# Recurrence outputs written to the other row halves and issued in turn with the state's update, and new starting rounds for attention's items

## The chip, the cores and the metric

One NeuronCore of a Trainium2 chip runs the whole program. The time is the device time of one execution in microseconds (us), as the median of several runs. TensorE (PE in the profile, PEld for its weight loads) multiplies, VectorE (DVE), ScalarE (ACT) and GpSimd (POOL) work on vectors, SyncE (SP) issues DMAs. Each engine works off its own instructions in program order, and engines wait for one another by semaphores.

## The reference

Two blocks follow each other. The first has two layers over 1,040 tokens (16 of them learned). In each layer an input projection feeds two branches: an attention with 4 heads over all tokens, and a recurrence over 8 heads with a state of 64 x 64, run once forwards and once backwards in time; both go through an output product and a norm, and then through a mixture of 32 experts. The second block has a differential attention, a gated spatial mixing and a gated feed-forward part. Everything is in 32-bit floats. The change concerns the first block's recurrence and the attention beside it:

```python
def step(S, inp):
    r_t, w_t, k_t, v_t, kk_t, b_t = inp
    sa = jnp.einsum('bhvk,bhk->bhv', S, kk_t)
    S = S * w_t[:, :, None, :] - sa[..., None] * b_t[:, :, None, :] + v_t[..., None] * k_t[:, :, None, :]
    return S, jnp.einsum('bhvk,bhk->bhv', S, r_t)

def attend(blk):
    qn, qp = blk
    s = jnp.einsum('bqhd,bkhd->bhqk', qn, k_nope) + jnp.einsum('bqhd,bkd->bhqk', qp, k_pe)
    p = jax.nn.softmax(s.astype(jnp.float32) * scale, axis=-1).astype(v.dtype)
    return jnp.einsum('bhqk,bkhd->bqhd', p, v)
```

## The kernel before, in words

The program runs stage after stage: projections, then recurrence with attention (some 350 to 1,085 us for layer 0, some 2,155 to 2,875 us for layer 1), closing products, routing, experts, and then the second block.

**The recurrence in chunks.** Time is cut into 10 steps of 104 tokens (C), each of two chunks of 52 (H), for each direction d (0 forwards, 1 backwards). Two heads lie above each other in the 128 partitions: one in rows 0 to 63, the other in rows 64 to 127; a chunk's tokens take rows 0 to 51 and 64 to 115 (these slices are `ODD`, line 1185). Within a chunk the recurrence is solved with matrices. A step has phases 0 to 31 (`PHASES`, line 1177): 0 makes the gate inputs from the low-rank weights (line 1365, called lora here); 1 to 10 make decays, exponentials and scaled keys, on VectorE, ScalarE and GpSimd; 11 and 14 turn matrices over; 12 and 13 make the products of keys; 15 to 25 invert a triangular matrix in five levels, each with a first part (T by lm, gives XX) and a second part (XX by T, gives T); 26 to 28 and 29 to 31 are the two chunks: the right-hand side (`state_rows`, evicted to rh), the solve (evicted to uu), and then, in phases 28 and 31, the state's update and the outputs.

**Rounds.** 23 groups of phases make a step. `rounds()` (line 1218) issues one group of direction 0 and one of direction 1 in a round, direction 1 being 11 rounds behind (`STAGGER`). So when direction 0 is in its group r, direction 1 is in group r + 12 (or r - 11). Between the two directions' parts of a round stands attention's turn (the entry with None). The order in a round is direction 0, attention, direction 1; in rounds 0 to 3 of direction 0's step it is direction 1, attention, direction 0, since a direction in its first four groups goes last. All engines take this same order. Phases 28 and 31 come in rounds 19 and 22 for direction 0 and in rounds 7 and 10 for direction 1. The gate inputs come in round 0 for direction 0 and in round 11 for direction 1. Direction 1's level four is in rounds 1 and 2 (first and second part), direction 0's in rounds 13 and 14; direction 0's round 12 is the second part of level three.

**State's update and outputs.** In `scan_pe` (line 1356), part 2, the update's products go as 16 matmuls: for each of 4 pairs of heads j two accumulated products (tm by vt, tm by uu), each for both row halves. They read rows of one half and write partitions of the same half, so a matmul of the upper half and one of the lower half make a pair. Then a semaphore step tells VectorE, which adds the update to S (line 1625). After that come the outputs (`outputs`, line 1336): for each j three accumulated products (S by kr, v by Ak, uu by Ab), again for both halves, 24 matmuls, in the same halves. ScalarE evicts them to ys (line 1475, `take` in `scan_act`), and `scan_sp` (line 1662) stores ys by four DMAs a step and direction. A 32-bit matmul shows as two instructions in the trace, so a pair shows as 4. `state_rows` and the five levels mix straight and crossed halves (`quarters`, line 1318).

**Attention's items.** An item is one tile of queries (104 in layer 0, 128 in layer 1) of one head: 40 items in layer 0, 32 in layer 1. It takes six rounds from its start (`att_turn`, line 1711): first round, scores of two of three spans of keys (kn by qn, kpe by qp); second, the third span, and on VectorE the three maxima (line 1837); third, the exponentials on ScalarE; fourth, the turning of p on TensorE (consts by p) and its copies; fifth, p by v (v by pT); sixth, the division o on VectorE (line 1862), its square on ScalarE (line 1826) and the store. `item_starts` (line 1683) takes the starting rounds within a step from `STARTS` (four items in a step; layer 0, and steps 0 and 5 of layer 1) or `FEWER` (three items; the other steps of layer 1). In step 0 the first start is left out.

Of the kernel before, what the change touches and what calls it, by code (L numbers as in the profile page):

```python
# [19 lines left out]
H, HP = 52, 116  # L20
# [188 lines left out]
class Program:  # L209
# [20 lines left out]
    def place(self, o, width, dt, name):  # L230
        if (o, width, dt, name) not in self.tensors:
            self.tensors[o, width, dt, name] = self.nc.alloc_sbuf_tensor_at(
                f"{name}{len(self.tensors)}", [128, width], dt, offset=self.base + 4 * o)
        return self.tensors[o, width, dt, name][:, :]
# [54 lines left out]
def mms(e, mats):  # L289
    for out, a, b, start, stop in mats:  # L290
        made = e.matmul(out, a, b, start=start, stop=stop)  # L291
    return made
# [890 lines left out]
MASKS = {14: 0, 15: 1, 16: 2, 18: 3, 20: 4, 22: 5}  # L1183
BY_ACT = {2, 3, 8, 9} | {13 + 3 * lv for lv in range(4)} | {25 + 4 * x + n for x in range(2) for n in (0, 1, 3)}
ODD = [(slice(64 * o, 64 * o + 64), slice(64 * o, 64 * o + H)) for o in range(2)]


def scan_mem(P):
# [49 lines left out]
def chunk(d, step):  # L1238
    i = step if d == 0 else NT - 1 - step
    return slice(C * i, C * i + C)  # L1240


def half(d, step, ch):
    t0 = chunk(d, step).start + H * ch
    return slice(t0, t0 + H)
# [6 lines left out]
def scan_bank(P, d, step, use):  # L1252
    return P.ps[2 * d + use % 2]
# [32 lines left out]
def half_rows(o):  # L1286
    return slice(64 * o, 64 * o + H)
# [7 lines left out]
def side(lv, ch, j):  # L1295

    return (j ^ ch * lv) & 1
# [12 lines left out]
def split_columns(j):  # L1312

    at = 128 * (j % 2) + 64 * (j // 2)
    return slice(at, at + 64)


def quarters(js):

    return [(j, o, half_rows(o), half_rows(o ^ j % 2)) for j in js for o in range(2)]  # L1320


def state_rows(P, d, m, S, ch, v):

    mats, hs = [], slice(H * ch, H * ch + H)
    for js in ((0, 1), (2, 3)):
        for j, o, r, x in quarters(js):
            out = P.ps[2 * d + j % 2][x, 64 * (j // 2):64 * (j // 2) + 64]
            mats.append((out, m.kr[64 * o:64 * o + 64, j, 0, hs], S[64 * o:64 * o + 64, j, :], True, False))
        for j, o, r, x in quarters(js):  # L1330
            out = P.ps[2 * d + j % 2][x, 64 * (j // 2):64 * (j // 2) + 64]
            mats.append((out, m.ak[r, place(1, ch, j), 0, :], v[r, 64 * j:64 * j + 64], False, True))
    return mats


def outputs(ps, m, S, ch, v):

    mats, hs = [], slice(H * ch, H * ch + H)
    for j in range(4):
        jc, u = slice(64 * j, 64 * j + 64), place(1, ch, j)  # L1340
        mats += [(ps[r, jc], m.kr[q, j, 1, hs], S[q, j, :], True, False) for q, r in ODD]
        mats += [(ps[r, jc], m.ak[r, u, 1, :], v[r, jc], False, False) for q, r in ODD]
        mats += [(ps[r, jc], m.ab[r, u, 1, :], m.uu[r, split_columns(j)], False, True) for q, r in ODD]
    return mats


def turns(e, P, pairs):

    made = []
    for out, a in pairs:  # L1350
        n, p = a.shape[0], a.base_partition()
        made.append((out, a, P.K["ident"][p:p + n, p:p + n], True, True))
    return mms(e, made)


def scan_pe(e, P, li, d, step, ph):
    rw, pe, dv, ac, po = P.rw, P.c("scan_pe"), P.c("scan_dve"), P.c("scan_act"), P.c("scan_pool")
    m, sl, key = P.scan[d], chunk(d, step), (li, d, step)
# [9 lines left out]
    if ph == 11:  # L1368
        e.wait_ge(*dv.at(*key, "kr0"))
        b = scan_bank(P, d, step, 2)  # L1370
        turns(e, P, [(b[r, 256 * ch + 64 * j:256 * ch + 64 * j + 64], rw.v[q, j, half(d, step, ch)])
                   for ch in range(2) for j in range(4) for q, r in ODD]).then_inc(*pe.tick(*key, 2))
    if ph in (11, 14):
        k, use = (1, 3) if ph == 11 else (0, 8)
        b = scan_bank(P, d, step, use)
        if ph == 14:
            scan_free(e, P, li, d, step, use)
        e.wait_ge(*dv.at(*key, f"hb{k}"))
        turns(e, P, [(b[r, 256 * ch + 64 * j:256 * ch + 64 * j + 64], m.hb[q, k, j, H * ch:H * ch + H])
                   for ch in range(2) for j in range(4) for q, r in ODD]).then_inc(*pe.tick(*key, use))  # L1380
    if 12 <= ph < 14:
        e.wait_ge(*dv.at(*key, "kr1" if ph == 12 else "hb0"))
        mat = 1 if ph == 12 else 0
        for ch in range(2):
            use = 2 * ph - 20 + ch
            b, hs = scan_bank(P, d, step, use), slice(H * ch, H * ch + H)
            scan_free(e, P, li, d, step, use)
            at = [2 * H * (place(1, ch, j) // 4 * 2 + j // 2) for j in range(4)]
            mms(e, [(b[r, at[j]:at[j] + 2 * H].rearrange("p (a t) -> p a t", a=2),
                     m.hb[q, mat, j, hs], m.kr[q, j, :, hs], True, True) for j in range(4) for q, r in ODD]  # L1390
                ).then_inc(*pe.tick(*key, use))
# [9 lines left out]
    if 16 <= ph < 26:  # L1401
# [3 lines left out]
        mats = []  # L1405
        if not second:
# [6 lines left out]
            for n in range(4):  # L1413
                for k in range(2):
                    ch, i = divmod(n, 2)
                    j = 2 * i + side(lv, ch, k)
                    for o in range(2):
                        r, x = half_rows(o), half_rows(o ^ k)
# [3 lines left out]
        else:  # L1422
            e.wait_ge(*dv.at(*key, "ev", base))
            for n in range(4 if lv < 5 else 0):
                for k in range(2):
                    ch, i = divmod(n, 2)
                    j = 2 * i + side(lv, ch, k)
                    for o in range(2):
                        r, x = half_rows(o), half_rows(o ^ k)
                        mats.append((left[r, k, H * n:H * n + H], m.TT[x, turned_place(lv, ch, j), :],  # L1430
                                     m.XX[x, 4 * k + n, :], True, True))
            for j in range(4):
                for ch in range(2):
                    for o in range(2):
                        x, y = half_rows(o ^ side(lv, ch, j)), half_rows(o ^ side(lv + 1, ch, j))
# [3 lines left out]
    if ph >= 26:  # L1439
        x, part = divmod(ph - 26, 3)  # L1440
        ch, S, use = m.chunks[x], m.S[x], 25 + 4 * x
        if part == 0:
            if x == 0:
                e.wait_ge(*dv.at(*key, "T", 5))
                e.wait_ge(*ac.at(*key, "T", 5))
                e.wait_ge(*ac.at(*key, "ev", 2))
                e.wait_ge(*dv.at(*key, "ev", 7))
            else:
                e.wait_ge(*ac.at(*key, "ev", use - 1))
            e.wait_ge(*(dv.at(*key, "fS", x) if step or x else dv.at(li, d, "S0")))  # L1450
            mms(e, state_rows(P, d, m, S, ch, m.vt[:, ch, :])).then_inc(*pe.tick(*key, use))
        if part == 1:
            e.wait_ge(*ac.at(*key, "ev", use))
            mms(e, [(P.ps[2 * d + j % 2][r, 64 * (j // 2):64 * (j // 2) + 64], m.TT[c, 4 * ch + j, :],
                     m.rh[c, split_columns(j)], True, True) for j, o, r, c in quarters(range(4))]
                ).then_inc(*pe.tick(*key, use + 1))
        if part == 2:
            b = scan_bank(P, d, step, use + 2)
            mats = []
            for j in range(4):  # L1460
                jc = slice(64 * j, 64 * j + 64)
                mats += [(b[q, jc], m.tm[r, 0, ch, jc], m.vt[r, ch, jc], True, False) for q, r in ODD]
                mats += [(b[q, jc], m.tm[r, 1, ch, jc], m.uu[r, split_columns(j)], False, True) for q, r in ODD]
            e.wait_ge(*ac.at(*key, "ev", use + 1))
            mms(e, mats).then_inc(*pe.tick(*key, use + 2))
            mms(e, outputs(scan_bank(P, d, step, use + 3), m, S, ch, m.vt[:, ch, :])).then_inc(*pe.tick(*key, use + 3))


def scan_act(e, P, li, d, step, ph):
# [192 lines left out]
def scan_sp(e, P, li, d, step, ph):  # L1662
    if ph == 31:
        e.wait_ge(*P.c("scan_act").at(li, d, step, "ev", 32))
        y = P.T[f"y{d}"][chunk(d, step), :].rearrange("(c t) (j o n) -> t o c j n", c=2, o=2, n=64)
        for o in range(2):
            for ch in range(2):
                e.dma_start(y[:, o, ch], P.scan[d].ys[64 * o:64 * o + H, ch, :].rearrange("p (j n) -> p j n", j=4)
                            ).then_inc(*P.d(f"scan_y{d}_out").tick(li, step, 2 * o + ch))


# [4 lines left out]

STARTS = (2, 8, 13, 20)
FEWER = (2, 9, 17)  # L1680


def item_starts(li):

    made = []
    for q in range(NT + 1):
        places = STARTS if li == 0 or q in (0, 5) else FEWER
        made += [STEPS * q + at for at in places if q or at != STARTS[0]]
    return made[:4 * TILES_OF[li]]
# [183 lines left out]
def recur_sp(e, P, li):  # L1873
    for o in range(2):
        e.dma_start(P.att.kpe[64 * o:64 * o + 64, :], P.T["kp"][:, 1 - o]).then_inc(
            *P.d("att_kpe_in").tick(li, *(() if o else ("hi",))))
    for piece in range(PIECES):
        att_load(e, P, li, 0, piece)
    att_query(e, P, li, 0)
    att_query(e, P, li, 1)  # L1880
    for piece in range(PIECES):
        att_load(e, P, li, 1, piece)
    for n, part in rounds():
        if part is None:
            att_sp(e, P, li, n)
            close_head_sp(e, P, li, n - STEPS * NT)
        else:
            scan_sp(e, P, li, *part)


def recur_pe(e, P, li):
    for n, part in rounds():
        if part is None:
            att_pe(e, P, li, n)
            close_head_pe(e, P, li, n - STEPS * NT)
        else:
            scan_pe(e, P, li, *part)
# [2513 lines left out]
```

## Time and profile before

| what | value |
|---|---|
| median of 3 runs | 4873.55 us (4872.19 to 4876.98) |
| profiled execution: time, span | 4854.41 us, 4852.5 us |
| PE busy, share of the span | 4436.8 us, 91% |
| DVE, ACT, POOL busy | 3122.8 us (64%), 2157.3 us (44%), 1191.1 us (25%) |
| mean granted clock of TensorE | 0.961 of full speed |
| layer 0, one step of the recurrence | 71.3 us |
| layer 1, one step of the recurrence (three items) | 67.9 us |

The span is the time from the first to the last instruction of the profiled execution. Busy shares are means over all stages. In the recurrence many small matmuls run at once and their ends are modelled, so the start of the next burst says more than the busy time.

### The profile page before, as it was taken

Reading aid. Unit: us, or ns where it says so; the run is one execution under the profiler, and the core shown is the slowest. Engines: PE = TensorE matmul, PEld = TensorE weight load, DVE = VectorE, ACT = ScalarE, POOL = GpSimd, SP = SyncE. Lnnn points to the kernel's source line nnn. Section 1 sums busy time; section 2 is a strip of 40 time slices with the busy share of each in tenths; the row PEclk is TensorE's granted clock in tenths of the full one; section 3 lists DMA queues with packets and bytes.
Section 4 is the critical chain, followed back from the end, with each engine's and each line's share of the span. In section 5 each row is a group of like instructions: output and inputs, shape, how many; then the busy total and the mean of one; then the engine's idle time right before and its main releaser. Section 6 shows DMA issues by size and latency. Waiting matters only on the chain. (4 is left out here: it accounts for less than half of the span.)

```text
span 4852.5 us, 125717 instructions
## 1 busy us (share of the span) xinstructions
PE 4436.8 (91%) x55312; PEld 3779.0 (78%) x55312; DVE 3122.8 (64%) x4912; ACT 2157.3 (44%) x3962; POOL 1191.1 (25%) x863
## 2 busy tenths in 40 slices
PE   6989999999799969989999888899979889999999
PEld 6888888887588858878888877788767557888887
DVE  6436666669688974346666677888774476651752
ACT  2333444442388853334343432788742252331431
POOL 1003222322244510012222221444321001222221
PEclk9999999999899979999999998999989789999999
DMA  5411111133466674321111133666651003333332
GB/s 150 144 54 36 35 28 34 25 88 85 161 257 256 243 213 121 105 60 24 30 34 31 25 119 115 225 248 251 232 177 35 9 19 113 96 112 109 113 113 91
DMA packets 385989, 535.77 MB, mean 110 GB/s; under 512 B 117982, under 2 KB 310558, under 8 KB 358422
## 3 DMA queue, kind: packets, MB, share of 16 engines
q1 hardware_dynamic: 343349, 488.54, 31.0%
q0 software_dynamic: 40752, 33.95, 2.2%
q8 instruction: 439, 7.19, 0.6%
q10 hardware_dynamic: 1344, 5.24, 0.3%
q14 instruction: 105, 0.85, 0.1%
HBM read 569.43 MB, written 121.40 MB: 142 GB/s over the span
## 5 line engine op out<-in xcount | busy, mean ns | idle before, releaser
L291 PE MATMUL ps<-w_hi,xbT 128*128 128x512 f32 x1520 | 497.5, 398 | 19.1 <-DVE w L2860 19.1
L291 PE MATMUL ps<-hT,w_in 128*128 128x416 f32 (+1 forms) x2736 | 493.1, 338 | 4.1 <-DVE hT L3147 4.1
L291 PEld LDWEIGHTS ps<-hT,w_in 128*128 128x128 f32 x2736 | 456.8, 194 | 30.0 <-issue 19.2
L2860 DVE TENSOR_TENSOR w<-w,w_hi 128x2048 fp32r<-128x2048 f32 x190 | 425.4, 2277 | 2.2 <-ACT w_hi L2817 2.2
L1657 POOL TENSOR_TENSOR lm<-Ab,consts 116x416 f32<-116x416 f32 x240 | 256.6, 1077 | 407.3 <-PE ps L291 237.3
L2817 ACT ACTIVATE w_hi<-w 128x2048 fp32r<-128x2048 f32 x190 | 355.2, 1935 | 0.0
L291 PEld LDWEIGHTS ps<-w_hi,xbT 128*128 128x128 f32 x1520 | 287.3, 189 | 86.4 <-DVE w L2860 28.1
L291 PE MATMUL ps<-w,xbT 128*128 128x512 f32 x760 | 297.9, 392 | 0.0
L2891 DVE TENSOR_TENSOR w<-w,w_hi 128x2048 fp32r<-128x2048 f32 x95 | 221.6, 2333 | 95.6 <-ACT w_hi L2853 95.6
L291 PE MATMUL ps<-w_hi,actT 128*128 128x512 f32 x760 | 250.8, 391 | 4.9 <-DVE actT L2886 4.9
L291 PE MATMUL ps<-x1T,w_gate 128*128 128x512 f32 x1056 | 249.5, 392 | 3.0 <-DVE x1T L3834 1.6
L291 PE MATMUL ps<-x1T,w_up 128*128 128x512 f32 x1056 | 246.5, 389 | 0.0
L291 PE MATMUL ps<-w_down,act 128*128 128x512 f32 x1056 | 241.6, 391 | 2.8 <-POOL w_down L4060 2.8
L1600 DVE TENSOR_TENSOR XX<-ps,consts 116x416 f32<-116x416 f32 x200 | 117.4, 587 | 189.3 <-PE ps L291 189.0
L291 PEld LDWEIGHTS ps<-x1T,w_gate 128*128 128x128 f32 x1056 | 200.0, 190 | 45.6 <-issue 1.9
L291 PEld LDWEIGHTS ps<-w_down,act 128*128 128x128 f32 x1056 | 199.3, 189 | 44.9 <-POOL w_down L4060 3.3
L291 PEld LDWEIGHTS ps<-x1T,w_up 128*128 128x128 f32 x1056 | 198.2, 188 | 41.2
L4051 POOL TENSOR_TENSOR w_up<-w_up,w_up 128x1024 fp32r<-128x1024 f32 x44 | 116.4, 2646 | 458.0 <-ACT w_up L3973 458.0
L291 PE MATMUL ps<-w_out,mixT 128*104 128x512 f32 (+1 forms) x864 | 218.5, 407 | 10.4 <-DVE w_out L2198 5.8
L2806 POOL DMA_INDIRECT t_ys<-yo,slots x95 | 101.3, 1066 | 461.5 <-PE ps L298 371.0
L291 PEld LDWEIGHTS ps<-w_out,mixT 128*104 128x104 f32 (+1 forms) x864 | 152.0, 179 | 67.5 <-DVE w_out L2198 9.6
L794 POOL TENSOR_TENSOR w_in<-w_in,w_in 128x1024 fp32r<-128x1024 f32 x22 | 56.0, 2551 | 598.9 <-ACT w_in L809 598.9
(464 smaller groups left out, 10776.2 us busy)
## 6 DMA issues: line engine op xcount, KB each, us to landing
w<-in_moe_w_dram SPq DMA_DIRECT2D x192, 1024.0 KB, 12.4
w_gate<-in_w_gate_dram SPq DMA_DIRECT2D x44, 512.0 KB, 3.8
w_up<-in_w_up_dram SPq DMA_DIRECT2D x44, 512.0 KB, 3.8
w_down<-in_w_down_dram SPq DMA_DIRECT2D x44, 512.0 KB, 3.6
w_in<-in_w_in_dram SPq DMA_DIRECT2D x36, 512.0 KB, 4.2
w_out<-in_w_out_dram SPq DMA_DIRECT2D x24, 512.0 KB, 8.3
t_h<-x SPq DMA_DIRECT2D x20, 416.0 KB
kn<-t_kn SPq DMA_DIRECT2D x32, 260.0 KB, 3.6
```

The costliest lines, as they stand in the source:

```text
L291: made = e.matmul(out, a, b, start=start, stop=stop)
L794: e.tensor_tensor(w.lo, w.x, w.hf, ALU.subtract).then_inc(*count.tick(li, "lo", n))
L1600: e.tensor_tensor(m.XX[0:HP].rearrange("p (k u) t -> p k u t", k=2), both_banks(P, d, 0)[0:HP].rearrange("p k (u t) -> p k u t", t=H), bc( ...
L1657: e.tensor_tensor(m.LM[lv % 2][0:HP], m.ab[0:HP, :, 0, :], bc(m.lmask[0:HP, H * lv:H * lv + H].unsqueeze(1), [HP, 8, H]), ALU.mult).then_i ...
L2806: e.indirect_dma_start(T["ys"], bass.IndirectOffsetOnAxis(P.slots[:, table_column(b - 2):table_column(b - 2) + 1], 0), m.yo[b % 2], None, ...
L2817: e.activation(w.hi, w.x, ACT.Copy).then_inc(*P.c("moe_act").tick(li, "w13", b, k))
L2860: e.tensor_tensor(w.lo, w.x, w.hf, ALU.subtract).then_inc(*P.c("moe_dve").tick(li, "w13", b, k))
L2891: e.tensor_tensor(w.lo, w.x, w.hf, ALU.subtract).then_inc(*dv.tick(li, "w2", b))
L4051: e.tensor_tensor(w.lo, w.x, w.hf, ALU.subtract).then_inc(*po.tick(0, c, "lo", f))
```

## The change

The outputs of a direction's chunk are written to the other row half: the products that read rows 0 to 63 now write partitions 64 to 115, and those that read rows 64 to 127 write partitions 0 to 51 (`CROSSED`). The stores of ys take the halves the other way round. The update and the outputs are no longer issued one after the other: a pair of the update is followed by a pair of the outputs, seven times; then comes the last pair of the update, with its semaphore step, and then the last five pairs of the outputs. And attention's items start in rounds 2, 7, 13 and 19 of a step instead of 2, 8, 13 and 20, or, where there are three, in 2, 7 and 19 instead of 2, 9 and 17.

```diff
+CROSSED = [(slice(64 * o, 64 * o + 64), slice(64 * o, 64 * o + H), slice(64 - 64 * o, 64 - 64 * o + H)) for o in range(2)]
...
-        mats += [(ps[r, jc], m.kr[q, j, 1, hs], S[q, j, :], True, False) for q, r in ODD]
-        mats += [(ps[r, jc], m.ak[r, u, 1, :], v[r, jc], False, False) for q, r in ODD]
-        mats += [(ps[r, jc], m.ab[r, u, 1, :], m.uu[r, split_columns(j)], False, True) for q, r in ODD]
+        mats += [(ps[x, jc], m.kr[q, j, 1, hs], S[q, j, :], True, False) for q, r, x in CROSSED]
+        mats += [(ps[x, jc], m.ak[r, u, 1, :], v[r, jc], False, False) for q, r, x in CROSSED]
+        mats += [(ps[x, jc], m.ab[r, u, 1, :], m.uu[r, split_columns(j)], False, True) for q, r, x in CROSSED]
...
+            outs = outputs(scan_bank(P, d, step, use + 3), m, S, ch, m.vt[:, ch, :])
             e.wait_ge(*ac.at(*key, "ev", use + 1))
-            mms(e, mats).then_inc(*pe.tick(*key, use + 2))
-            mms(e, outputs(scan_bank(P, d, step, use + 3), m, S, ch, m.vt[:, ch, :])).then_inc(*pe.tick(*key, use + 3))
+            for k in range(0, len(mats) - 2, 2):
+                mms(e, mats[k:k + 2] + outs[k:k + 2])
+            mms(e, mats[len(mats) - 2:]).then_inc(*pe.tick(*key, use + 2))
+            mms(e, outs[len(mats) - 2:]).then_inc(*pe.tick(*key, use + 3))
...
-                e.dma_start(y[:, o, ch], P.scan[d].ys[64 * o:64 * o + H, ch, :].rearrange("p (j n) -> p j n", j=4)
+                e.dma_start(y[:, 1 - o, ch], P.scan[d].ys[64 * o:64 * o + H, ch, :].rearrange("p (j n) -> p j n", j=4)
...
-STARTS = (2, 8, 13, 20)
-FEWER = (2, 9, 17)
+STARTS = (2, 7, 13, 19)
+FEWER = (2, 7, 19)
```

## Rows read from the trace of the kernel before

**Rows 1.** Busy time by stretch: one step of each layer

```profile
core 0: us, PE busy (x) PEld busy (x) DVE busy (x) ACT busy (x) POOL busy (x), PEclk, DMA share, GB/s
644.39:715.72 71.33, 67.75 (x2008) 61.38 (x2009) 46.48 (x113) 30.25 (x89) 20.11 (x21) 1.00 0.12 27
2303.21:2371.15 67.94, 62.63 (x1966) 56.87 (x1967) 43.90 (x103) 28.19 (x79) 20.49 (x21) 1.00 0.13 31
```

**Rows 2.** Timeline, layer 0, round 7: start, length, instruction, count, idle before

```profile
653.26 0.19 PEld L291 LDWEIGHTS ps<-vT,hbT 52*64 52x64 f32 x4 [0.25 <-ACT uu L1475]
...
654.19 0.19 PEld L291 LDWEIGHTS ps<-S,kr 64*52 64x52 f32 x4
...
655.50 0.53 PEld L291 LDWEIGHTS ps<-XX,T 52*52 52x52 f32 x29
```

**Rows 3.** Timeline of weight loads, layer 0, round 8: the right-hand side

```profile
658.29 0.19 PEld L291 LDWEIGHTS ps<-S,kr 64*52 64x52 f32 x8 [0.24 <-issue]
...
658.74 0.49 PEld L291 LDWEIGHTS ps<-T,lm 52*52 52x52 f32 x32
```

**Rows 4.** Timeline, layer 0, rounds 8 to 11: attention's pieces

```profile
656.52 0.42 PEld L291 LDWEIGHTS ps<-kn,qn 128*104 128x104 f32 x3
...
659.28 0.41 PEld L291 LDWEIGHTS ps<-kn,qn 128*104 128x104 f32 x3
...
659.93 1.36 DVE L1837 TENSOR_REDUCE stat<-ps 104x1 f32<-104x348 f32 x3
...
660.24 0.30 PEld L291 LDWEIGHTS ps<-rh,T 52*52 52x52 f32 x16 [0.23 <-issue]
...
664.29 0.81 PEld L298 LDWEIGHTS ps<-consts,p 104*116 104x116 f32 x9
...
665.24 0.18 PEld L1365 LDWEIGHTS ps<-u,w 64*128 64x128 f32 x1
```

**Rows 5.** Timeline of layer 0, rounds 1 to 3, from lora's end

```profile
702.94 0.59 DVE L1536 TENSOR_TENSOR sig<-ps,par 128x416 f32<-128x416 f32 x1 [0.60 <-PE ps L1365]
...
703.49 2.21 PE L291 MATMUL ps<-v,pT 116*104 116x128 f32 x18
...
705.63 0.60 PE L291 MATMUL ps<-XX,T 52*52 52x52 f32 x32
...
707.46 0.58 DVE L1608 COPY T<-ps 116x416 f32<-116x416 f32 x1
...
708.31 0.60 PE L291 MATMUL ps<-T,lm 52*52 52x52 f32 x32
...
708.65 0.53 ACT L1486 ACTIVATE ei<-cs 128x416 f32<-128x416 f32 x1
```

**Rows 6.** Timeline of weight loads, layer 1, rounds 1 to 3, from lora's end

```profile
2360.20 0.48 PEld L291 LDWEIGHTS ps<-T,lm 52*52 52x52 f32 x32
...
2365.51 0.51 PEld L291 LDWEIGHTS ps<-T,lm 52*52 52x52 f32 x32 [1.09 <-ACT ei L1486]
```

**Rows 7.** Timeline of layer 0, rounds 12 to 14, from lora's end

```profile
666.31 0.60 PE L291 MATMUL ps<-XX,T 52*52 52x52 f32 x32
...
670.93 0.58 DVE L1600 TENSOR_TENSOR XX<-ps,consts 116x416 f32<-116x416 f32 x1
...
671.67 0.60 PE L291 MATMUL ps<-XX,T 52*52 52x52 f32 x32
```

**Rows 8.** Timeline of weight loads, layer 0, round 22 to round 0

```profile
699.60 0.48 PEld L291 LDWEIGHTS ps<-XX,T 52*52 52x52 f32 x32 [0.84 <-DVE XX L1600]
```

**Rows 9.** Timeline of weight loads, layer 1, rounds 12 to 14, from lora's end

```profile
2463.99 0.48 PEld L291 LDWEIGHTS ps<-XX,T 52*52 52x52 f32 x32
...
2470.47 0.48 PEld L291 LDWEIGHTS ps<-XX,T 52*52 52x52 f32 x32 [1.43 <-DVE XX L1600]
```

**Rows 10.** Timeline of weight loads, layer 1, round 17 to round 0

```profile
2340.38 0.45 PEld L291 LDWEIGHTS ps<-kn,qn 128*128 128x128 f32 x3
...
2345.61 0.20 PEld L291 LDWEIGHTS ps<-vT,hbT 52*64 52x64 f32 x4
...
2358.20 0.48 PEld L291 LDWEIGHTS ps<-XX,T 52*52 52x52 f32 x32 [0.85 <-DVE XX L1600]
```

## The prediction

> **What bounds the kernel now.** I read four views: busy time by stretch, the timeline of TensorE's weight loads, the waits of TensorE, and the timeline of VectorE and ScalarE. In the recurrence TensorE is what counts: in one step of layer 0, 23 rounds and 71.33 us long, its matmuls are busy 67.75 us, in one of layer 1 62.63 of 67.94 [rows 1]. The granted clock is 1.00 in both (the upper level, 2.4 GHz), so the clock is no part of this. TensorE takes its bursts in program order, so a step lasts as long as its bursts plus the waits between them: a shorter burst is worth its full length, unless the next burst then waits for something else. So I price each burst, and then look for what is late next in every round that the new starts empty.
>
> A round runs direction 0's burst, attention's piece, direction 1's burst (in rounds 0 to 3 direction 1 comes first). Between one burst of a direction and its next stands an eviction. With nothing in between, that hand-over shows as a wait of 0.84 us [rows 8], some 0.9 with the pipeline's end. Attention's pieces are what fills it. An item has four on TensorE: scores A (its first round, two spans: 656.52 to 658.29, 1.77 us), scores B (second, 0.96), the turning T (fourth, 0.95) and PV (fifth, 2.14) [rows 3 to 5].
>
> **The outputs, crossed.** State's update is 8 pairs of matmuls in 0.93 us, outputs 12 pairs in 1.31 [rows 2]: 0.116 and 0.109 a pair, 2.24 together. Can four go in the time of a pair? The right-hand side (phase 29) does so already, over both row halves and both column halves: four sets of four in 0.45 us, 0.113 a set [rows 3]. After: 7 sets at 0.116, one pair of the state, 5 of the outputs: 0.81 + 0.12 + 0.54 = 1.47. That is 0.77 less in each of 4 places a step. State's update ends as late as before (7 sets and a pair, 0.93), so its reader on VectorE gains nothing. Bounds: from 0 (the sets run as pairs) to 1.31 (all outputs hidden); I take 0.77, since rows 3 have the same shape. The eviction to ys and its four stores come earlier with nobody waiting; swapping halves in the store costs nothing, as the packets stay the same.
>
> The Trainium skill, "TensorE: Matmul & The Clock Gate", section "Part 3: Packing small matmuls", says that a weight load overlaps running matmuls only if they use another group of rows. The crossed outputs share their rows with the update, so by this the saving would be 0; rows 3 (8 loads of four matmuls every 0.11 us, two per row half) speak against it.
>
> **The new starts, layer 0.** With four items a step, item 2 begins in round 7 instead of 8 and item 4 in 19 instead of 20. So A goes from 8 to 7 and 20 to 19, B from 9 to 8 and 21 to 20, T from 11 to 10 and 0 to 22, PV from 12 to 11 and 1 to 0. Emptied: 1, 9, 12, 21. No burst is added, so the question is what each emptied round gives back.
>
> *Rounds 1 and 12.* In the round before, the other direction's gate inputs (line 1365, "lora") were made. From there VectorE works off nine operations without a gap: in round 1 from sig at 702.94 to T at 707.46, done at 708.04, and the burst that reads T starts at 708.31, just after [rows 5]. PV, 703.49 to 705.63, lies inside this window. Layer 1 has the same rounds without PV, and there they take 2360.20 to 2365.51, 5.31 us, against 5.37 with it (702.94 to 708.31) [rows 5, 6]. So PV is free there today. Round 12 is alike: 666.31 to 671.67, 5.36 us, and XX, the last of VectorE's chain, is done at 671.51, 0.16 before [rows 7]. After the change PV stands ahead of lora, in rounds 0 and 11, where TensorE waits for nothing, and costs 2.14. The windows give back 0.1 to 0.2 and lose 0.26, since the item's division o (fifth piece's eviction) now falls into the chain. Net +2.2 each, +4.4 a step. Bounds: 0 (the window shrinks by all of PV) to +2.4.
>
> *Rounds 9 and 21.* B, 0.96, is paid in rounds 8 and 20 instead. What comes back? Round 9 today takes 658.74 to about 660.5, 1.75 us [rows 3, 4]. Emptied, the burst (0.45) and the hand-over (0.9) make at least 1.35. But the three maxima of the scores, 1.36 us on VectorE [rows 4], now stand a round earlier and ahead of this XX, which puts the next burst at about 1.7. So nearly nothing comes back: +0.9 each, +1.8 (bounds +0.5 and +1.1 each).
>
> *Gains.* A in round 7 fills the 0.25 us that the update waits for uu [rows 2]: -0.25. The item that began in 20 now ends in round 1, not 2, so its square on ScalarE no longer stands ahead of the exponential ei, which starts at 708.65 though its input is there by about 707.5, just ahead of T [rows 5]. The chain from ei to round 5 comes some 0.8 earlier (bounds 0 and 1.1): -0.8. T's two moves cost and give 0.95 each: 0. SP's and POOL's queues get nothing new: a query's loads are issued two items ahead.
>
> Sum a step: -3.1 + 4.4 + 1.8 - 0.25 - 0.8 = +2.05. Of ten steps, the first has no item in round 0: 9.5 x 2.05 = +19.
>
> **Layer 1.** Two of its ten steps have four items: +4. Eight have three, moved from 9 and 17 to 7 and 19. Rounds 7 to 14: two crossings -1.54; T from 12 to 10, +1.0; PV from 13 to 11, +2.14; the window that they leave takes 6.48 today, longer since the item's own copies stand in VectorE's chain [rows 9], and 5.36 + 0.26 after: -0.86; waits filled in 7 and 8, less a new one in 9: -0.3. That is +0.4. Rounds 17 and 18 lose A and B: 5.23 us from A to the update [rows 10] become about 2.7 (what stays, and 0.25 for uu): -2.5. Rounds 19 to 22, 12.59 [rows 10]: +1.8 A, +1.0 B and a wait of 1.0 in round 21, against -2.14 PV, -0.4 of waits for exponentials and -1.54: about -0.2 with the rest. PV in round 0: +2.15. The chain of rounds 1 to 3: +0.25. Sum +0.1, eight times: +1.
>
> **Together** +19 + 4 + 1 = +24 us. The profiled execution took 4854.4 (span 4852.5 and 1.9 around it); it would become 4878. The runs shown have a median of 4873.55, 19 above the profiled one, so I put the change on that: 4898. A difference below 0.2% (9.7 us) I count as none.
>
> **Rivals.**
> *W, the windows close.* Rounds 1 and 12 fall to the bare hand-over of 0.9 instead of some 2.2 idle. For it: VectorE's chain begins when lora ends, and only its last operations are read so late. Against: rows 6. It decides from 0.8 us given back in each of the 30 windows that lose PV (19 in layer 0, 11 in layer 1; 24 / 30); the full 1.3 would be -39: 4859, faster. Half of it is no change.
> *N, the pieces are neutral.* The starts cost nothing anywhere, and the crossing alone tells: 80 x 0.77 = -62, 4812, faster. For it: the same work on the busiest engine. Against: rows 5 to 7, where it lies beside VectorE's work.
> *H, the tail hides too.* The five last pairs run on crossed halves alone, so the next burst could start beside them: up to 0.54 more in 80 places, -43: 4855. Against: in rows 2 the next burst starts only as the outputs end.
> *P, the sets run as pairs.* The crossing saves nothing: 4898 + 62 = 4960. Against: rows 3.
>
> **Chances.** Forecast 0.58 (4884 to 4915); W 0.16, half of it faster; N 0.10; H 0.07; P 0.04; the rest, 0.05, is no change. Slower: 0.58 + 0.04, and 0.03 of W's weak end: 0.65. Faster: 0.08 + 0.10 + 0.07 = 0.25. Same: 0.10. The forecast's own range takes the ends of rounds 9 and 21 and of ei (-1.1 to +0.8 a step). The range for 8 in 10 goes from 4838 (N's lower half and little else left out) to 4925.
>
> **What would show it.** Right: a step of layer 0 near 73.4 us and of layer 1 near 68; state and outputs in 1.5 us with 14 outputs between the update's; TensorE idle some 1.2 us in round 1 and 1.3 in round 12, before the bursts that wait for XX and T, and again one round later; lora's end to the fourth burst after it still 5.3 to 5.6; new waits for XX in rounds 9 and 21; no wait for uu in round 7; ei about 0.8 earlier against lora. Wrong: those windows at 4 us or less (W), a step of layer 0 below 70 (N), outputs at no extra time (H), or an update that takes 1.5 us or more (P).

## The result and the profile after

The changed kernel takes 4925.9 us (median of 4 runs, 4919.1 to 4931.7) against 4873.2 before: 1.0114 times as long, 95% interval 1.0102 to 1.0126, 52.7 us slower where 24 were forecast. The profiled execution took 4919.1 us, its span 4917.2, with a granted clock of 0.953.

One step of each layer, by stretch, as in [rows 1]:

```profile
core 0: us, PE busy (x) PEld busy (x) DVE busy (x) ACT busy (x) POOL busy (x), PEclk, DMA share, GB/s
639.47:712.16 72.69, 64.34 (x2008) 57.79 (x2008) 46.78 (x112) 30.41 (x86) 20.09 (x20) 1.00 0.13 29
2466.02:2538.75 72.73, 61.23 (x1968) 55.19 (x1967) 44.67 (x102) 28.43 (x77) 20.03 (x20) 0.98 0.12 27
```

From a layer's first gate product to its last eviction of outputs, layer 0 takes 756.7 us (735.4 before) and layer 1 755.6 (717.2). So in the profiles layer 0 lost 21, much as forecast (19), and layer 1 38 instead of 5. The profiled execution of before lies 19 us under its median, so layer times compared with it can look too long: here they add up to 60, where the medians are 53 apart.

State and outputs in layer 0, round 7, on TensorE; the answer to [rows 2] (start, length, instruction, count):

```profile
663.00 0.27 PE L291 MATMUL ps<-vT,hbT 52*64 52x64 f32 x2
663.01 0.26 PE L291 MATMUL ps<-S,kr 64*52 64x64 f32 x2
...
664.07 0.28 PE L291 MATMUL ps<-S,kr 64*52 64x64 f32 x4
664.18 0.22 PE L291 MATMUL ps<-vT,Ak 52*52 52x64 f32 x2
664.19 0.25 PE L291 MATMUL ps<-XX,T 52*52 52x52 f32 x2
```

Update and outputs start together. The next burst starts 1.19 us after the first product, between the last outputs; before it was 2.24. The wait for uu is gone. The same part in round 22:

```profile
704.09 0.23 PE L291 MATMUL ps<-vT,hbT 52*64 52x64 f32 x2
...
704.92 0.28 PE L291 MATMUL ps<-uu,hbT 52*64 52x64 f32 x3
706.13 0.27 PE L291 MATMUL ps<-uu,hbT 52*64 52x64 f32 x1 [0.94 <-issue]
```

Here TensorE stops for 0.94 us with nothing in the profile that it waits for ("issue"). Below, idle time of TensorE of this kind is called issue idle, or a stall. What became of [rows 5, 7], rounds 12 to 14 and 1 to 3 of layer 0, on the weight loads:

```profile
675.60 0.48 PEld L291 LDWEIGHTS ps<-XX,T 52*52 52x52 f32 x32
...
677.83 0.48 PEld L291 LDWEIGHTS ps<-T,lm 52*52 52x52 f32 x32 [1.37 <-ACT T L1479]
...
681.12 0.48 PEld L291 LDWEIGHTS ps<-XX,T 52*52 52x52 f32 x32 [1.22 <-DVE XX L1604]
...
713.24 0.48 PEld L291 LDWEIGHTS ps<-T,lm 52*52 52x52 f32 x32
714.98 0.48 PEld L291 LDWEIGHTS ps<-XX,T 52*52 52x52 f32 x32 [1.26 <-DVE XX L1604]
...
718.81 0.51 PEld L291 LDWEIGHTS ps<-T,lm 52*52 52x52 f32 x32 [1.39 <-ACT ei L1490]
```

The windows last 5.52 and 5.57 us (5.36 and 5.37 before): PV is gone from them and they stand as long, with the waits where the prediction put them. Layer 1, rounds 12 to 14, the answer to [rows 9], and the same stretch by the granted clock (PEclk, third from the end):

```profile
2430.80 0.48 PEld L291 LDWEIGHTS ps<-XX,T 52*52 52x52 f32 x32
...
2433.03 0.48 PEld L291 LDWEIGHTS ps<-T,lm 52*52 52x52 f32 x32 [1.37 <-ACT T L1479]
2436.31 0.78 PEld L291 LDWEIGHTS ps<-XX,T 52*52 52x52 f32 x32 [2.80 <-DVE XX L1604]
...
2437.65 1.79 PEld L291 LDWEIGHTS ps<-consts,u 64*52 64x52 f32 x32
```

```profile
2425.00:2431.80 6.80, 6.79 (x217) 6.21 (x215) 3.35 (x9) 1.32 (x4) 0.00 (x0) 1.00 0.14 29
2431.80:2436.30 4.50, 0.60 (x32) 0.48 (x32) 4.36 (x11) 1.97 (x7) 2.62 (x3) 0.79 0.34 84
2436.30:2441.20 4.90, 4.89 (x136) 4.89 (x138) 2.26 (x7) 3.38 (x9) 1.06 (x1) 0.50 0.02 3
2441.20:2446.00 4.80, 4.46 (x149) 4.18 (x143) 3.73 (x8) 1.04 (x3) 2.67 (x3) 1.00 0.02 3
```

The same rounds before:

```profile
2466.20:2470.40 4.20, 2.88 (x50) 2.56 (x50) 4.06 (x10) 0.94 (x2) 2.28 (x3) 1.00 0.34 72
2470.40:2473.30 2.90, 2.71 (x125) 2.58 (x126) 2.57 (x9) 2.84 (x8) 0.38 (x1) 1.00 0.13 28
```

The window closes to 5.51 as forecast (6.48 before). But TensorE was busy for 0.60 of 4.50 us (2.88 of 4.20 before), and the next 4.90 us run at 0.50, the lower of its two levels: 32 loads that take 0.48 us take 0.78. Round 14 lasts 4.4 us in the mean of such steps, 2.8 before.

### The profile page after: what moved, and what is told of

Same layout as the page of the kernel before. It is cut to its first block and busy times, and to the rows that moved or that the text cites. A ratio compares the mean times of both kernels' runs of the same rounds, so it can differ in the third digit from the quotient of the medians.

```text
span 4917.2 us, 125717 instructions
## 1 busy us (share of the span) xinstructions
PE 4406.4 (90%) x55312; PEld 3741.6 (76%) x55312; DVE 3125.9 (64%) x4912; ACT 2161.7 (44%) x3962; POOL 1187.2 (24%) x863
## 5 line engine op out<-in xcount | busy, mean ns | idle before, releaser
L291 PE MATMUL ps<-w_hi,xbT 128*128 128x512 f32 x1520 | 497.5, 398 | 19.3 <-DVE w L2864 19.3
L2774 POOL DMA_INDIRECT xb<-t_h,toks x95 | 185.1, 1949 | 64.2 <-DVE toks L2582 35.8
```

The source lines that it names most:

```text
L2774: e.indirect_dma_start(out, None, table, bass.IndirectOffsetOnAxis(idx, 0), bounds_check=bound, oob_is_err=False).then_inc(*into.tick(li, b))
```

## The experiments

Two questions: is the loss the new starts' (theory S) with the crossing saving its 62 us, and if not, what ate it?

**The two parts, each alone.** `e1_crossing`: the changed kernel with the old starts. `e2_starts`: the kernel before with the new ones.

```diff
-STARTS = (2, 7, 13, 19)
-FEWER = (2, 7, 19)
+STARTS = (2, 8, 13, 20)
+FEWER = (2, 9, 17)
```

> The crossing alone, with the starts of before (2, 8, 13, 20 and 2, 9, 17). Theory S (the crossing saves, the starts cost): 80 places at 0.77 to 1.0 us, 62 to 80 us less than before, 4793 to 4811; the granted clock stays at 0.96. Rival I (the interleaved sets run into TensorE's instruction supply, and the idle time without a wait inside them, which grew by 13 us in the changed kernel, is the crossing's own): 50 us less at the most, about 4825. Rival P (sets run as pairs): no change, 4873.

> The new starts alone (2, 7, 13, 19 and 2, 7, 19), outputs uncrossed and behind the update as before. Theory S: the changed kernel without its saving, 62 to 80 us above it, 4988 to 5006. Rival C (the starts and the crossing belong together: the longer update and outputs fill what the crossed kernel leaves idle in round 12): 30 us above the changed kernel, about 4955.

Measured: the crossing alone 0.9978 of before (0.9959 to 0.9997), 4857.7 against 4870.4: 13 us saved. The starts alone 1.0197 (1.0180 to 1.0214), 4963.3: 93 lost, 86 by the prediction's sum without its 62. On the new starts the crossing saves 0.83%, 40 us. So the starts cost about what was forecast, and the crossing, which saved 13 us and 40 us, fell short of its 62, as rival I of `e1_crossing` had it. Rival C of `e2_starts` (starts and crossing belong together) came nearer to 4963 than theory S, but it falls with `e1_crossing`: by it the crossing would save more on the old starts, and it saves less. The waits of TensorE in layer 0 (us in total, times, longest), before, crossing alone, starts alone, changed:

```profile
PE ps L291 <- issue: 5.8, 15, 1.3
```

```profile
PE ps L291 <- issue: 27.9, 31, 2.0
```

```profile
PE ps L298 <- issue: 1.5, 2, 1.0
...
PE ps L291 <- issue: 0.4, 2, 0.2
```

```profile
PE ps L291 <- DVE XX L1604: 41.5, 48, 2.5
PE ps L291 <- ACT T L1479: 12.4, 10, 1.2
...
PE ps L291 <- issue: 8.1, 13, 1.9
...
PE ps L298 <- issue: 2.8, 3, 1.7
```

Both layers, all lines: issue idle grows from 10.3 to 48.9 us with the crossing on the old starts, from 4.0 to 26.9 on the new. 40 saved and 23 of new idle make the 62. TensorE's busy time in the two layers says the same: with the crossing it falls by 60 us on the new starts (1358.1 to 1298.2), by 47 on the old (1334.8 to 1288.1), where the granted clock of layer 0, from its start to its end, falls from 0.98 to 0.96.

**One half of the new starts undone**, `e3_four` with FEWER and `e4_three` with STARTS as before.

> The changed kernel, but the steps with three items keep the starts of before (2, 9, 17). Eight steps of layer 1 differ from the changed kernel. Theory S with the loss in the three-item steps: these take 71.8 us in the changed kernel and would take 68.4 less 3.1 to 4.0, so 6.4 to 7.4 less, eight times: 50 to 60 less than the changed kernel, 4866 to 4876, and the granted clock of layer 1 stays at 1.00 in rounds 13 to 15. Rival K (layer 1's loss is in its steps' hand-over or its clock whatever the starts): 25 less at the most, 4900 or more.

> The changed kernel, but the steps with four items keep the starts of before (2, 8, 13, 20): ten of layer 0 and two of layer 1. Theory S: a step of layer 0 takes 72.0 us in the changed kernel and would take 70.3 less 3.1 to 4.0, so 4.8 to 5.7 less, 11.5 times: 55 to 66 less than the changed kernel, 4860 to 4871. Rival N (in layer 0 the pieces are neutral and only layer 1 loses): 4920 or more.

Measured: 1.0033 (1.0018 to 1.0047), 0.8% or 39 us less than the changed kernel, and 1.0057 (1.0040 to 1.0075), 28 less. Both layers lose by the starts, so K and N fall. Each gives back less than expected; that fits the crossing's saving less on the old starts, but was not tested by itself.

**Which edit of the crossing saves.** `e10_uncrossed` (the stores' halves put back too) and `e11_sequence`, both on the old starts:

```diff
-CROSSED = [(..., ..., slice(64 - 64 * o, 64 - 64 * o + H)) for o in range(2)]
+CROSSED = [(..., ..., slice(64 * o, 64 * o + H)) for o in range(2)]
```

```diff
-for k in range(0, len(mats) - 2, 2):
-    mms(e, mats[k:k + 2] + outs[k:k + 2])
...
+mms(e, mats).then_inc(*pe.tick(*key, use + 2))
+mms(e, outs).then_inc(*pe.tick(*key, use + 3))
```

> The crossing alone, with the outputs back in their own halves but still issued in turn with the update. Theory H (four products run side by side only if each has a quarter of rows and columns to itself; here two of a set of four want the same quarter): state and outputs take 2.24 us as before, the update is done up to 0.9 later for its reader: 4870 to 4900. Rival W (weight loads and products of the two alternate freely, and it is the taking in turn that saves): as the crossing alone, 4858, with state and outputs in 1.4 us.

> The crossing alone, with crossed outputs but issued behind the whole update as before. Theory H: a pair of outputs still fills two of the four quarters and nothing of the update is left to run beside it: 2.24 us and 4870. Rival W2 (the crossing as such saves, since its weights go to rows that the pair before did not use): state and outputs in 1.8 us or less, 4858 or less.

Measured: 1.0004 (0.9994 to 1.0013) and 0.9988 (0.9979 to 0.9998). From first to last product the part takes 2.28 us taken in turn without crossing, 2.11 crossed in sequence (one set overlaps at the seam), 1.36 with both. Weight loads of the first in round 7:

```profile
656.67 0.19 PEld L291 LDWEIGHTS ps<-vT,hbT 52*64 52x64 f32 x4 [0.25 <-ACT uu L1479]
656.78 0.19 PEld L291 LDWEIGHTS ps<-S,kr 64*52 64x52 f32 x4
656.90 0.20 PEld L291 LDWEIGHTS ps<-uu,hbT 52*64 52x64 f32 x4
```

Each pair waits its 0.11 us. So H holds in the main: taking in turn alone saves nothing, crossing alone the 0.17 us at the seam (6 us in all, 0.12%), and the 0.9 us need both.

**Where the stalls lie.** The page has, for the queue that brings TensorE's instructions (packets, MB):

```profile
q8 instruction: 439, 7.19, 0.6%
```

That is 16 KB a packet. TensorE's 55,312 loads, as many matmuls and 1,742 separate waits and drains are 112,366 instructions, 256 a packet. Number them along this stream and divide by 256: on the weight loads all 31 stalls over 0.35 us between 360 and 1,050 us of the crossing alone, and 30 of 37 such idle times of layer 1's recurrence, leave one and the same remainder (give or take two). The kernel before has such idle times at this place too, 16 in layer 0, five of them over 0.35 us. In the trace most packets land 0.9 to 1.4 us after they start, the stalled engine goes on 1.3 to 1.6 after the last landing, and from one such place to the next pass 3.5 us (median where it stalled). Without the stall these 31 stretches of 256 would have taken 1.8 to 3.7 us (median 2.4); of the 121 that did not stall, eight took under 3.1. So a stretch that runs faster mostly waits for its successor; state and outputs alone are 160 instructions in 1.36 us. To test it, a step of layer 0 (4,052 instructions) was filled up to 4,096, so that these places stand still, and shifted as a whole. Two of the waits in the edit make one instruction.

```diff
+if ph == 13 and d == 0:
+    for _ in range(2 * PADS.get((li, step), 0)):
+        e.wait_ge(*dv.at(*key, "kr1"))
...
+for _ in range(2 * BEFORE[li]):
+    over(e, P, 0, EMBED[0])
```

> The crossing alone with the starts of before, and 43 or 44 waits that are already met put on TensorE ahead of round 5's product of each step of layer 0, so that a step has 4096 instructions instead of 4052, sixteen times 256; and 129 of them ahead of the layer, so that a step's first instruction lies 168 ahead of a place where the engine was seen to stall. Theory F (the stalls without a wait come at every 256th instruction of TensorE's stream, where the next 256 have not arrived, if the 256 before took under 3.2 us): worked out from the times between instructions in the crossing alone, 1.2 us of stalls a step instead of 3.1, in nine steps 17 less, given back in part by the added instructions (0 to 12): 4841 to 4853, and stalls in layer 0 of 12 us instead of 31. Rival A (the stalls follow the interleaved sets and not the place in the stream): stalls as in the crossing alone, 4858 to 4870.

> The same instructions as in the kernel with 129 waits ahead of the layer, but with 229, so that a step's first instruction lies 68 ahead of such a place. Theory F: 4.6 us of stalls a step, 31 more than the other in nine steps, 4872 to 4884. Rival A: the same time as the other.

Measured: 1.0073 (1.0061 to 1.0085), 4907.0, and 1.0199 (1.0186 to 1.0212), 4971.6: 65 apart with the same steps. In the profiles 39 are layer 0's (781.1 and 820.4 us), 14 stand ahead of it, with the 100 more waits, and 14 are layer 1's, whose place moved too. Rival A falls, but not by the number alone, and 4841 to 4853 was wrong: the 44 waits hold TensorE for 4.6 us a step, 0.1 apiece. `e9_aligned` has products in the place of the waits:

```diff
+if ph == 13 and d == 0 and li == 0:
+    mms(e, [(P.ps[7][0:64, 256:272], spare, spare[:, 0:16], True, True)] * (11 if step else 43))
```

> The crossing alone with the starts of before, a step of layer 0 again filled up to 4096 instructions and begun 168 ahead of a place where TensorE's stream was seen to stall, but with 11 small products that nobody reads (four instructions each) where TensorE waits 1.3 us in round 5, in place of waits that took 0.1 us apiece; 32 more of them stand in the first step. Theory F (instruction supply): stalls in layer 0 of some 2.3 us a step, as in the kernel with the same place and 129 waits ahead, against 3.1, and none of the 4.6 us that the waits took; 5 to 15 less than the crossing alone: 4843 to 4853. Rival A (the place in the stream tells nothing): 4858 or more.

Measured: 0.9978 (0.9969 to 0.9987), 4862.3, no gain over the crossing alone, and by the number rival A's. Issue idle of layer 0 fell from 29.6 to 20.6 us and nine steps got 6 shorter together, but the first got 11 longer by its 43 products, and layer 1, in another place, takes 717.9 against 707.3 (in `e13_mix` below, in the same place as the crossing alone, it takes 715, so the place explains a part of this at most).

A cleaner pair, on the changed kernel: the same number of instructions before layer 1, only the step's place in layer 0 differs (48 products in the first step and 11 in the last, or 10 and 49).

```diff
+if ph == 23 and d == 0 and li == 0:
+    mms(e, [... for n in range({0: 48, NT - 1: 11}.get(step, 11))])
```

> The changed kernel with 11 small products that nobody reads (four instructions each) at the start of round 14's burst of direction 0, where TensorE waits for VectorE, in each step of layer 0 (48 in the first): a step has 4096 instructions and begins 111 ahead of a place where TensorE's stream was seen to stall. Theory F: stalls in layer 0 of 4 us in nine steps, against 9.3 in the changed kernel; the products lie in the wait: 4917 to 4926. Rival A: layer 0 as in the other kernel of this pair.

> The same with 10 products in the first step and 49 in the last, so that all is the same from the end of layer 0 on, but the steps begin 7 ahead of such a place. Theory F: 1.6 to 2.1 us more of stalls a step, layer 0 longer by 14 to 19 than in the other kernel: 4932 to 4945. Rival A: the same time as the other.

Measured: 1.0129 (1.0112 to 1.0146), 4935.5, and 1.0182 (1.0168 to 1.0196), 4962.3: 27 us by the place alone, layer 0 757.0 and 786.9. By the medians of eight steps, rounds 22 and 0 grow by 1.4 and 2.0 us; of the rest only rounds 8 and 10 differ by over 0.2, and they cancel. Rounds 22 and 0 of one step, good place, TensorE's timeline and clock:

```profile
711.29 0.28 PE L291 MATMUL ps<-uu,Ab 52*52 52x64 f32 x4
711.50 1.02 PE L298 MATMUL ps<-consts,p 104*116 104x104 f32 x9
...
714.79 2.21 PE L291 MATMUL ps<-v,pT 116*104 116x128 f32 x18
```

```profile
713.70:716.90 3.20, 3.13 (x82) 2.97 (x82) 0.60 (x2) 0.52 (x1) 0.00 (x0) 1.00 0.30 62
```

And the bad place:

```profile
722.04 0.28 PE L291 MATMUL ps<-uu,Ab 52*52 52x64 f32 x3
723.93 0.26 PE L291 MATMUL ps<-uu,Ab 52*52 52x64 f32 x1 [1.61 <-issue]
724.11 1.01 PE L298 MATMUL ps<-consts,p 104*116 104x104 f32 x9
...
726.38 0.88 PE L291 MATMUL ps<-XX,T 52*52 52x52 f32 x32 [0.71 <-DVE XX L1608]
...
727.88 3.20 PE L291 MATMUL ps<-v,pT 116*104 116x128 f32 x18
```

```profile
726.40:731.00 4.60, 4.60 (x82) 4.37 (x82) 0.59 (x1) 0.52 (x1) 0.00 (x0) 0.63 0.18 41
```

The last output waits 1.61 us for its instruction. Then, with the wait for XX that both have, the clock falls, and PV takes 3.20 us instead of 2.21. So a stall costs itself and often the clock behind it: in the bad place round 0 runs at 0.54 to 0.70 in seven of nine steps, in the good place at 1.00 in all nine. Forecast were 14 to 19 for the stalls alone (4932 to 4945 in all), and 4962.3 lies above that. Issue idle of layer 0 grew by 11 (7.6 to 18.6), and TensorE's busy time, with the same instructions, by 15 (668.6 to 683.9, the clock 0.98 and 0.95): together 26 of the 30. The good one's own time missed too (4917 to 4926 expected): layer 0 is as in the changed kernel, layer 1, moved, 9 longer.

**The clock in layer 1.** `e5_fill` puts products that nobody reads into the idle time of rounds 12 and 13.

```diff
+if li == 1 and q in (1, 2, 3, 4, 6, 7, 8, 9) and g in (12, 13):
+    mms(e, [(P.ps[4][:, 0:tn], kpe[:, 0:128], kpe[:, t0:t0 + tn], True, True)] * (5 if g == 12 else 13))
```

> The changed kernel, with products that nobody reads put into TensorE's idle time of rounds 12 and 13 in the three-item steps of layer 1 (5 and 13 of 128 by about 400, some 0.9 and 2.3 us; the two waits there are 1.24 and 2.68). Theory K (the idle time pulls the granted clock to 0.50, and rounds 14 to 16 pay for it): the clock stays at 1.00 there, round 14 goes from 4.4 to 2.9 us, eight times 1.5: 12 less than the changed kernel, about 4914. Rival D (the clock is a by-product, rounds 14 to 16 wait for VectorE anyway): no change, 4926. Rival L (the added products delay the burst behind them): above 4930.

Measured: 1.0099 (1.0085 to 1.0114), 4926.1: not told apart from the changed kernel, the number that rival D gave. The mechanism of K is there all the same: with the window still 5.52 us long, what follows runs at

```profile
2448.20:2453.10 4.90, 4.72 (x197) 4.59 (x199) 3.57 (x11) 3.91 (x11) 1.07 (x1) 1.00 0.02 5
```

and round 14 takes 2.84 us instead of 4.43. But the mean step fell by only 1.0, as rounds 22 and 0 took 0.6 more; issue idle of layer 1 went from 16.0 to 21.3 us. That the added instructions moved its stalls is likely, not shown. Layer 0, with the very instructions of the changed kernel, took 767 us instead of 757: such differences between two executions hide effects of this size.

**PV's place.** `e12_late` is the changed kernel with PV one round later for the items that begin in rounds 7 and 19; `e13_mix` has FEWER as before besides.

```diff
+            late = (n - k) % STEPS in (7, 19)
+            if k != (4 if late else 6):
+                found.append((k - 1 if late and k > 4 else k, ITEM_STARTS[li].index(n - k)))
```

> The changed kernel with PV, and what reads it, one round later for the items that begin in rounds 7 and 19: PV back in rounds 12 and 1, beside VectorE's chain, A, B and T where the change put them. Theory V (PV, 2.14 us, is free in these rounds and paid in rounds 11 and 0, the prediction's largest term): 4.4 less a step in 9.5 steps of layer 0 and in its two kin of layer 1, 4.3 in eight of layer 1: 86 less than the changed kernel, 4840; less of it if the instruction supply takes a part, as it took of the crossing: 4840 to 4870. Rival W (the emptied rounds have closed by most of PV): within 20 of the changed kernel, 4906 or more.

> The crossing; in steps of four items the starts of the change with PV one round later for those of rounds 7 and 19; in steps of three the starts of before (2, 9, 17). Theory V (what each part gave in its own kernel adds up): layer 0 as in the changed kernel with the late PV, 733.8 us, layer 1 as in the crossing alone, 707.3, together 11.5 less than the 735.4 and 717.2 of before in the profiles, and 16 less than the crossing alone with its 740.0 and 707.3: 4840 to 4850. Rival A (another place in the stream takes it back, as in the kernel filled up with products): 4858 or more.

Measured for `e12_late`: 1.0005 (0.9996 to 1.0014), 4874.2: 52 less than the changed kernel, so W falls. It is less than 86: rounds 11 to 14 of layer 0 give back 1.7 a step, rounds 0 to 4 1.4 (the item ends later again, and ei with it, which the expectation forgot), and issue idle of layer 0 grows from 10.9 to 17.9 us. The mix: 0.9971 (0.9960 to 0.9982), 4860.6; the parts did not add up to 4845, and the number is rival A's. Its layer 0 has the very instructions of the late PV's and took 740.0 us instead of 733.8, with a granted clock of 0.97 instead of 0.98: so the miss does not show that the place in the stream took the rest.

`e8_windows` tries PV in the windows of layer 1 on the old starts, with FEWER = (2, 8, 20).

> The crossing with the starts of before in the steps of four items, and 2, 8, 20 instead of 2, 9, 17 in those of three, so that PV lies in rounds 12 and 1 in layer 1 too. Theory V (PV is free beside VectorE's chain there, as the prediction had it for layer 0): rounds 8 to 13 of layer 1 take 16.9 us before and 16.1 in layer 0 with that start, rounds 16 to 0 take 25.1 against 24.1 without the item of round 13: 1.8 less a step, eight steps, 14 less than the crossing alone: about 4843. Rival Q (two pieces of scores close behind a crossed update run into TensorE's instruction supply, or the clock falls in the emptied rounds): no gain, 4858 or more.

Measured: 1.0020 (1.0010 to 1.0031), 20 more than the crossing alone. Rival Q: issue idle of layer 1 is 34.4 us instead of 19.3, the granted clock there 0.97 instead of 0.99.

Of all kernels the crossing alone, `e9_aligned` and the mix are the fastest, 0.2 to 0.3% below before and not told apart.

## Why the prediction was wrong

Point by point, by its own steps:

- **Rounds 1 and 12** (+4.4 a step): the waits came as described and the windows stayed (5.52, 5.57, and 5.51 in layer 1). Putting PV back gave 3.1 a step in layer 0, where 4.4 less 0.8 for ei would be 3.6. Right, a little large.
- **Rounds 9 and 21, uu, ei**: the waits for XX in rounds 9 and 21 are there (0.3 and 0.7 us), the wait for uu in round 7 is gone, and ei starts 4.99 us after lora's end instead of 5.71: 0.7, forecast 0.8.
- **Starts as a whole**: +86 forecast, +93 measured, but not where it was put: in the profiles layer 0 44.5 (49 forecast), layer 1 58 (36). These add up to 103, since the profiled execution of before was a fast one; layer 1 stays too dear even so: `e10_uncrossed`, as fast as before by its median, has 727 us there instead of 717.
- **The outputs, crossed** (-0.77 in 80 places, -62): the step that failed first. Where nothing stalls the term is there, and rather too small: the next burst comes 1.04 earlier in rounds 7 and 10, 0.93 in 19 and 22 (starts alone against changed), so rival H is half true. But 40 us arrived on the new starts and 13 on the old. What is missing is the instructions: the sum counted TensorE's time by row halves and never asked whether its instructions arrive. That the stalls come at every 256th instruction, and that shifting them costs 27 us in one layer, is shown. On the new starts the idle time that is new (23 us) covers what is missing of the 62 (22), on the old 39 of 49; the clock's fall in layer 0 (0.97 in the recurrence, 0.99 before) is the likely rest.
- **Layer 1, "+0.4" for rounds 7 to 14**: the second step that failed, since it put the clock's part at nothing. The window shrank as said (-0.97; forecast -0.86), and round 14 gave 1.6 to 1.8 back at half the clock. "So the clock is no part of this" was read off a kernel whose idle times were short, and the change lengthened them to 1.4 and 2.8 in a row. Refilling them mended the clock but not the time, so its price in the whole, and with it the cause of layer 1's surplus, is open.

That layer 0 came out near its forecast (+19, in the profiles +21) proves little: the starts look 4 too dear and the crossing 6 too good, errors that cancel and that are no larger than what two executions of a layer differ by.

The Trainium skill, "TensorE: Matmul & The Clock Gate", section "Part 3: Packing small matmuls", says that a weight load overlaps running matmuls only if its row group differs. By this sentence alone the crossing would save nothing; 1.36 against 2.28 us says otherwise here: the rows are shared in both kernels, and only the half that the outputs are written to differs. Another page of the Trainium skill bears on what was missed: "Runtime: NRT & Kernel Launch", section "Instruction fetch mechanics", has TensorE's stream fetched in blocks of 256 instructions, the next while one runs, and calls the cost of a block's end "mostly hidden". The blocks agree with 439 packets; hidden it is not, at 31 stalls of 0.4 to 2.1 us in one layer.

## What to carry to other kernels

When many small matmuls are made faster, count the instructions of a burst beside its time: here 256 in under some 3 us mostly left TensorE waiting for its own stream, and moving the instructions alone, with the same work, cost half a per cent. Idle time without a wait inside a burst is the sign to look for; it stood in the trace of before. Price a change on an engine not only where it saves, but where it leaves the engine idle: idle times that follow each other can cost the clock of the next burst. And where two large terms cancel in a forecast, the sum can look right for the wrong reason, so test each alone, and compare differences of single stages with how much a stage differs between executions.

## What was not expected of the hardware

Stalls without any wait at each 256th TensorE instruction, up to 2 us; a separate wait on TensorE's queue holding it for 0.1 us even when met; the granted clock at 0.50 after 4.5 us with 0.60 busy, and at 0.63 in the mean of a burst after 1.61 and 0.71 us of idle time close together; and layer times that differ by 6 to 10 us between two executions of the same instructions.
